# Twelve input projections moved from the joined attention-and-recurrence steps into a new stage with the memory's and samples' attentions

## The reference, cut to what matters

```python
SPLITS = (D_RNN, D_RNN, NSA_HEADS * NSA_HD, 3 * 2 * NSA_KV * NSA_HD, 3 * NSA_HEADS, MEM_HEADS * MEM_HD, N_BRANCH * D_MODEL)
def project(x, p):
    z = rmsnorm(x, p['norm_mix']) @ p['w_in']
    ...
    merge = jax.nn.sigmoid(mg.reshape(B, T, N_BRANCH, D_MODEL))
    return lru_x, lru_gate, q, cmp_kv, sel_kv, win_kv, nsa_gates, mem_q, merge
...
def prompt_layer(x, mem, table, p):
    lru_x, lru_gate, q, cmp_kv, sel_kv, win_kv, ngate, mq, merge = project(x, p)
    o_lru, conv_new, h_new = lru_branch(lru_x, lru_gate, ...)
    ...
    o_nsa = lax.map(block, jnp.arange(T // Q_BLOCK, dtype=jnp.int32))
    ...
    o_mem = mem_attend(mq, mkv)
    y = merge_ffn(x, o_lru, o_nsa, o_mem, merge, p)
```

## Time and profile before

| | us |
|---|---|
| median of 3 runs | 2673.55 (2670.8 to 2675.91) |
| the profiled execution | 2671.46 |
| its span | 2669.8 |
| joined steps (from 376.0) | to 1333.6 |
| last stage, to the tail's first matmul | 1333.6 to 1614.0 |
| tail | 1614.0 to the end |

### The profile page before, as it was taken

How to read it: one execution, slowest core, us unless ns; L and a number is a source line. 1 busy time by engine, 2 the same in 40 slices (tenths; PEclk the granted TensorE clock), 3 DMA queues, 4 the chain that set the end, 5 groups by cost and what they waited for, 6 DMA issues and landing times. The chain is left out here.

```text
span 2669.8 us, 37831 instructions
## 1 busy us (share of the span) xinstructions
PE 2416.7 (91%) x14415; PEld 2234.0 (84%) x14415; DVE 1072.0 (40%) x1945; ACT 724.7 (27%) x1319; POOL 655.0 (25%) x399
## 2 busy tenths in 40 slices
PE   7996877989989899899856587999999999999999
PEld 7995647789888788799733577999999999999999
DVE  5465014436255564655433003263333333333333
ACT  5222011242352544644332004232211111111111
POOL 2212001111111011010035001234444434433443
PEclk9997789999999899999678568999999999999999
DMA  5224424224233221110056626332111111111112
GB/s 178 88 80 168 125 72 147 67 67 128 64 97 88 74 63 52 60 49 28 6 125 181 160 65 246 104 119 91 61 48 47 40 47 47 47 39 47 47 47 79
DMA packets 136151, 226.26 MB, mean 85 GB/s; under 512 B 29418, under 2 KB 95098, under 8 KB 135420
## 3 DMA queue, kind: packets, MB, share of 16 engines
q1 hardware_dynamic: 122492, 194.57, 23.5%
q0 software_dynamic: 6560, 25.22, 3.2%
q10 hardware_dynamic: 6976, 4.79, 0.7%
HBM read 176.80 MB, written 55.08 MB: 87 GB/s over the span
## 5 line engine op out<-in xcount | busy, mean ns | idle before, releaser
L1101 PE MATMUL att_facc<-h_hi,att_w_hi 128*128 128x344 f32 x960 | 337.7, 352 | 57.8 <-DVE att_zf L1281 44.5
L2153 PE MATMUL tl_acc<-tl_x_hi,tl_w_hi 128*128 128x344 f32 x1632 | 348.0, 322 | 21.1 <-DVE tl_x_lo L2216 14.0
L2153 PE MATMUL tl_acc<-tl_x_lo,tl_w_hi 128*128 128x344 f32 x1632 | 347.2, 321 | 0.0
L2153 PE MATMUL tl_acc<-tl_x_hi,tl_w_lo 128*128 128x344 f32 x1632 | 345.4, 320 | 0.0
L1101 PE MATMUL att_facc<-h_lo,att_w_hi 128*128 128x344 f32 x960 | 314.5, 328 | 0.0
L1101 PE MATMUL att_facc<-h_hi,att_w_lo 128*128 128x344 f32 x960 | 314.2, 327 | 0.0
L2153 PEld LDWEIGHTS tl_acc<-tl_x_hi,tl_w_hi 128*128 128x128 f32 x1632 | 275.2, 189 | 22.5 <-issue 15.9
L2153 PEld LDWEIGHTS tl_acc<-tl_x_lo,tl_w_hi 128*128 128x128 f32 x1632 | 277.0, 189 | 0.0
L2153 PEld LDWEIGHTS tl_acc<-tl_x_hi,tl_w_lo 128*128 128x128 f32 x1632 | 272.6, 188 | 0.0
L2118 POOL TENSOR_TENSOR tl_w_lo<-tl_raw,tl_w_hi 128x1024 fp32r<-128x1024 f32 x64 | 153.9, 2404 | 425.1 <-ACT tl_w_hi L2059 425.1
L1101 PEld LDWEIGHTS att_facc<-h_hi,att_w_hi 128*128 128x128 f32 x960 | 187.7, 196 | 72.4 <-DVE att_zf L1281 42.2
(11 more groups left out here) (355 smaller groups left out, 4031.5 us busy)
## 6 DMA issues: line engine op xcount, KB each, us to landing
tl_raw<-in_w_ff SPq DMA_DIRECT2D x66, 512.0 KB, 3.6
z<-att_zf SPq DMA_DIRECT2D x120, 172.0 KB, 3.7
att_raw<-in_w_in SPq DMA_DIRECT2D x40, 512.0 KB, 4.3
tl_tmp<-z SPq DMA_DIRECT2D x24, 516.0 KB, 4.4
tl_raw<-in_w_up SPq DMA_DIRECT2D x16, 512.0 KB, 4.0
fr_raw<-in_w_in SPq DMA_DIRECT2D x14, 512.0 KB, 4.8
zn<-fr_x SPq DMA_DIRECT2D x10, 516.0 KB, 2.9
fr_x<-in_xT SPq DMA_DIRECT2D x8, 644.0 KB, 10.3
```

Source lines behind the costliest of these rows:

```text
L1101: mm = pe.matmul(facc[:, 0:CW], w[:, u % 2, k, :], h[:, k, c * CW:(c + 1) * CW], start=(x == 0), stop=(x == 23))
L2153: mm = pe.matmul(a[:, c, 0:CW], wt[:, s, k, :], x[:, x0, c * CW:(c + 1) * CW], start=first and n == 0, stop=last and n == 2)
```

## The change

- Of the 40 filler units 12 (`FILL`, 144 ticks) leave the joined steps; there 28 units (336 ticks) stay, dealt out as (3, 2) in turn in the first three query tiles and (2, 1, 1, 1) afterwards, done by about step 178. The weights of the first two of the 12 are loaded and split in the joined steps.
- Within a joined step TensorE now does values and transposes (and turns) ahead of the filler ticks; ScalarE does `copies` ahead of `probs`; VectorE does accumulate, maxima and coefficient ahead of the evictions.
- The 24 output copies move into the joined steps: GpSimd issues one in each of the steps 24 to 47.
- The last stage becomes one function, `memory_and_samples`, whose matmuls carry the 12 units as fillers: 4 ticks at its beginning, 2 in each of the 32 memory steps, 3 with the scores of each of the 8 sequences, 2 at the selection, 1 with each of 8 memory scores, 2 at the transposes, 3 with the values of each sequence, 2 with the memory values of each. They have the one PSUM bank 7 (`facc`). The memory attention's loop is written out.
- In this stage SyncE alone loads all pages, window keys and values, and memory keys and values of the samples, through a ring of ten slots in a fixed order (`ITEMS`); an item waits until its slot's former item has been read. SyncE has the constants too. ScalarE issues the later query tiles' loads and the stores of `o_mem`; GpSimd loads, splits and stores the fillers.

```diff
+FILL = 12
...
-    UNITS += list(range(U_MG, NU_IN))
-    NU = len(UNITS)
+    NU = len(UNITS) + NU_IN - FILL - U_MG
+    UNITS += list(range(U_MG, NU_IN - FILL + 2))
+    raw, w_hi, w_lo, zf = fill
     PRE = 24
-    TICKS = ((4,),) * 3 + ((2, 2, 2, 1, 1) * 4 + (2,) * 4,) * (QT - 3)
+    TICKS = ((3, 2),) * 3 + ((2, 1, 1, 1),) * (QT - 3)
...
+                if 0 <= J - COPY < len(copies):
+                    dst, src, slow = copies[J - COPY]
+                    pool.dma_start(dst, src, allow_slow_non_contiguous=slow).then_inc(c_out, 16)
...
-                for tick in ticks[J]:
-                    filler(tick)
                 if J >= 1:
                     values(J - 1)
                 transposes(J)
...
                     turn(J // NJ - 1, 1)
+                for tick in ticks[J]:
+                    filler(tick)
...
-                    if J + 1 < NST:
-                        probs(J + 1)
                     copies(J)
...
+                    if J + 1 < NST:
+                        probs(J + 1)
...
+                if 2 <= J < NST + 2:
+                    accumulate(J - 2)
+                if J < NST:
+                    maxima(J)
+                if 1 <= J <= NST:
+                    coefficient(J - 1)
                 for g in range(3 * NU):
                     if chunk_at[g] + 1 == J and J:
                         evict(g)
-                if J < NST:
-                    maxima(J)
-                if 2 <= J < NST + 2:
-                    accumulate(J - 2)
-                if 1 <= J <= NST:
-                    coefficient(J - 1)
...
+def memory_and_samples(nc, d, per, h_hi, h_lo, fill):
...
+    NR, NJ = 10, MH * QT
...
+    DEAL = {"begin": 4, "mat": 2, "ks": 3, "grp": 2, "km": 1, "turn": 2, "vs": 3, "vm": 2}
...
+    for b in range(0, NS, 2):
+        ITEMS += [("ks", b), ("ks", b + 1), ("kw", b)]
+    ITEMS += [("km", b) for b in range(NS)]
+    for b in range(0, NS, 2):
+        ITEMS += [("vs", b), ("vs", b + 1), ("vw", b)]
+    ITEMS += [("vm", b) for b in range(NS)]
...
+            def ring_load(i):
+                kind, b = ITEMS[i]
+                slot, landed = ring[:, i % NR], r_in[i % NR]
+                if i >= NR:
+                    was, of = ITEMS[i - NR]
+                    read = {"k": mk_mm if was == "km" else k_mm, "v": mo_mm if was == "vm" else o_mm}[was[0]]
+                    sp.wait_ge(read, of + (2 if was[1] == "w" else 1))
+                if kind in ("ks", "vs"):
...
+                    with sp.Fori(0, PAGES) as x:
+                        page = sp.value_load(pt[0:1, bass.ds(x + b * PAGES, 1)], min_val=0, max_val=src.shape[0] - 1)
...
+            for m in range(QT):
+                constants(m)
+                for i in range(loaded, min(NR, loaded + 2)):
+                    ring_load(i)
+                    loaded += 1
+            for i in range(loaded, len(ITEMS)):
+                ring_load(i)
...
             for j in range(NJ):
                 if j + 1 < NJ:
...
                     values(j - 1)
                 turn(j)
+                filler(("mat", j))
             values(NJ - 1)
...
+            for b in range(NS):
+                sample_scores(b)
+                filler(("ks", b))
...
+            for b in range(NS):
+                memory_scores(b)
+                filler(("km", b))
...
+            for b in range(NS):
+                sample_values(b)
+                filler(("vs", b))
...
+            for b in range(NS):
+                memory_values(b)
+                filler(("vm", b))
```

More of the change, by code:

```diff
@@ L1007, in _ @@
             q_low(0, 0)
-            for u in range(2, NU):
+            for u in range(2, NU + 2):
                 if unit_at[u - 2] == -1:
@@ L1405, in _ @@
                     evict(g)
-def memory_attention(nc, d, per, ctx, block, bank, between):
+def memory_and_samples(nc, d, per, h_hi, h_lo, fill):
+    raw, w_hi, w_lo, zf = fill
+    UNITS = list(range(NU_IN - FILL, NU_IN))
     SC = P ** -0.5
[L1414 to L1438, removed]
@@ new lines, in _, with filler @@
+        @block.tensor
+        def _(pe):
+            def filler(p):
+                for tick in ticks[p]:
+                    u, c, g, x0 = tick // 12, tick // 4 % 3, tick // 4, 6 * (tick % 4)
+                    if tick % 12 == 0 and u >= 2:
+                        pe.wait_ge(f_lo, u - 1)
+                    if x0 == 0 and g:
+                        pe.wait_ge(f_ev, g)
+                    for x in range(x0, x0 + 6):
+                        k = x // 3
+                        w, h = ((w_hi, h_hi), (w_hi, h_lo), (w_lo, h_hi))[x % 3]
+                        mm = pe.matmul(facc[:, 0:CW], w[:, u % 2, k, :], h[:, k, c * CW:(c + 1) * CW],
+                                       start=(x == 0), stop=(x == 23))
+                    if x0 == 18:
+                        mm.then_inc(f_mm, 1)
@@ new lines, in _, with chain, evict @@
+        @block.vector
+        def _(dve):
+            n = [0]
+            def chain(ins):
+                n[0] += 1
+                ins.then_inc(ch, 1)
+                dve.wait_ge(ch, n[0])
+            def evict(p):
+                for g in chunks[p]:
+                    if g >= 4:
+                        dve.wait_ge(f_out[g % 4], 16 * (g // 4))
+                    c = g % 3
+                    dve.wait_ge(f_mm, g + 1)
+                    dve.tensor_tensor(zf[:, g % 4], facc[:, 0:CW], per["rstd"][:, c * CW:(c + 1) * CW], ALU.mult).then_inc(f_ev, 1)
@@ new lines, in memory_queries @@
+            def memory_queries(part):
+                if part == 0:
+                    chain(dve.memset(mqb[:], 0.0))
+                    dve.wait_ge(mc_in, 16)
+                q0 = mqb[:].rearrange("p n c -> p (n c)")
+                for x in range(8 * part, 8 * part + 8):
+                    ins = dve.tensor_copy(q0[:, x * (RP + 1):x * (RP + 1) + 1], mqs[:, x % MH, x // MH:x // MH + 1])
+                if part == 3:
+                    ins.then_inc(mqb_done, 1)
+            evict(("begin", 0))
@@ new lines, in _ @@
+                if j:
+                    evict(("mat", j - 1))
+                if j == 16:
+                    sample_queries()
+                if j in (18, 20, 22, 24):
+                    memory_queries((j - 18) // 2)
+            evict(("mat", NJ - 1))
+            for b in range(NS - 1):
+                evict(("ks", b))
+            dve.wait_ge(k_mm, NS)
+            dve.wait_ge(b_in, 16 * 2 * NS)
+            chain(dve.tensor_copy(lc[:, 0:40], S3[0:RW, 2:42]))
+            chain(dve.tensor_tensor(lc[:, 40:NCMP], S3[0:RW, 42:2 + NCMP], b_cmp[:], ALU.add))
```

765 lines of the change are left out of this document (393 added, 372 removed).

## The result

The changed kernel takes 2701.75 us, the median of 19 runs, against 2673.03 for the kernel before on the same chips: ratio 1.0083, 95% interval 1.0059 to 1.0107. It is slower, outside the range of the prediction and on the other side. Its 19 times lie in two groups: 7 from 2678 to 2686 us, at a mean granted clock of 0.933 to 0.937, and 12 from 2695 to 2710, at 0.924 to 0.930. The kernel before has one group, 2667 to 2681. The profile of after is of the lower group (2678.02 us, span 2676.1); a second profile, of the upper group, is the first experiment.

The account below looks back on a forecast made before the run. TensorE was taken to bound the joined steps and the tail, with waits and a slow clock in the stage between. Joined steps -84 and last stage with gap +57 gave -27 from 2671.5: 2645 us, range 2600 to 2690.

Parts of the forecast that it names:

- Fillers taken out: Joined steps: 12 units, 144 ticks, leave; 136 us of PE work, thirds change by -102, -38 and +4 us.
- (a): Joined steps: 34 filler chunks ending inside a step's ticks lose 0.76 us each; 26 us, of which +20 taken.
- (b): Joined steps: scores-to-transposes chain of 3.2 us exceeds PE's 2.2 us cover in some steps; +20 us, bounds 0 and 50.
- (c): Joined steps: fewer ticks around the recurrence's sigmoid, square root and gelu; +12 us, bounds 0 and 30.
- (d): Joined steps: 24 more output copies on GpSimd are hidden; 0, at worst 10 us of late weights.
- (e): Last third of the joined steps: four more ticks cost PE 4 us but give a busier clock; 0 net.
- steps 1 to 3: Last stage: loads 13 us, memory attention until 128 us after the stage's start, last sample scores done at 174 us.
- E: Start of the last stage, at the end of the joined steps; times in that stage are counted from it.
- Step 5: Last stage: SyncE alone issues every page, 12.0 us an item; last window values land 276 us after the stage's start.
- Step 6: Last stage after the last page load: remaining values, transposes and memory values end 322 us after its start, +55 us.
- The gap: Between the last stage and the tail's first matmul: 14.0 us stays, +2 for the last filler's store.
- R2: Joined steps: chain over VectorE and ScalarE, not PE, becomes the bound; -50 there, +67 in last stage: 2688, chance 0.22.

Follow-up runs that it names:

- the first experiment: The changed kernel unaltered, run again for a second profile: 2704.23 us over four runs, the profile at 2706.29.
- the aligned ticks: Changed kernel with joined-step ticks (2, 2, 4) in the first three query tiles and (2, 1, 1) after, chunks ending with a step's last tick: 2705.7 us.

## Why the prediction was wrong

- **Fillers taken out (-136).** Right as work; TensorE's busy time fell by 117 only. The step that failed is the assumption behind it, that what remains runs at the old clock. No term of the sum stood for a lower clock in the first three tiles (0.98 to 0.92). It is 17 to 19 us, all that the steps gave back less than forecast (66 for 84).
- **(a) Evictions (+20).** Right. The places were as counted (27 and 6, for 27 and 7). The page's 44.5 and 52.5 hold waits for the recurrence too; without those over 1.5 us, the waits behind evictions in the steps went from 7.8 us to 27.1, by 19. Not all of it could be won back, as the aligned ticks showed.
- **(b) The chain (+20).** Right: 1.12 us in the wait shown, at 34 steps, 37.1 us in all, less the 14.3 that the values no longer wait for copies: +23.
- **(c) The recurrence (+12).** Waits of fillers or values over 1.5 us behind VectorE, which itself had stood behind the recurrence: nine places before and after, 28.7 and 33.8 us: +5. Idle time in all grew by 51 us, for 52 predicted. That the sum agrees so closely is in part luck, as (b) and (c) miss in opposite directions.
- **(d) Copies (0).** Right.
- **(e) The last tile (0 net).** 102.0 us in after against 96.3: four more ticks, with the new order, raised the clock from 0.77 to 0.79 only. The thought that ticks give the clock back was right, but not with four more: it came with 24 in the tile (90.3 us at 1.00), and spreading them was the largest gain of any single edit here.
- **Last stage, steps 1 to 3.** Right: memory scores at E + 13.1, sample scores at E + 127, the last scores done at E + 175 (128 and 174 predicted).
- **Step 5, pages.** Right within 6 us: last window at 1549.37, E + 282 (276 predicted). Splitting the pages between two issuing engines took 13.6 us off. By the Trainium skill, "DMA: Bandwidth & Descriptors", section "Issuing engines are not separate DMA queues", it would have saved the sequencer's time alone, which it calls usually small; here that time was the bound, and the row decided rightly.
- **Step 6.** Wrong: 46 us predicted behind the last page, 52 in the lower group (1549.37 to 1601.86), 77 in the upper. I had put 2.5 us for the slow clock "behind the waits"; in the upper group the clock stays low in the memory values without any wait. That is 24 us in 12 of 19 runs.
- **The gap.** 18.0 us instead of the 16.
- **The sum.** Joined steps -66 instead of -84, last stage and gap +72 instead of +57: +6 for the lower group; with 24 more for the upper one +30, near the median's +29. R2 had the sign, but not the mechanism: its mark, transposes waiting in nearly every step, was met at 34 of 192, and fillers taken out still gave back time. Its price, 2688, lay below the median, since it had no clock either, and the +67 in it for the last stage came from no step. The range ended at R2. The hard end of the joined steps, -50, was added up wrongly: with (a) at 20 and (b) to (d) at their hard bounds it is -136 + 20 + 50 + 30 + 10 = -26, and R2 would have stood at 2712, above the median.

What stays open: how the idle time and the lower clock share the loss in the first three tiles; no run held one while it changed the other. Why the memory values take the higher clock in some runs and the lower in others is open: the trace shows when the clock turns, not why.

## What to carry to other kernels

Before wide matmuls are moved out of a stage, read the granted clock of every stretch that has few of them, and price what remains at that clock; here a tile with 24 ticks was faster than with none. In this kernel filler paid most where the kernel's own matmuls are narrow, spread evenly. A sum of engine work bounds the gain only until the chain of one step is reached: leaving most of the filler out took 245 us of matmuls away and brought 65.

## What the runs showed of the hardware

TensorE's clock can stay low without any idle time that the profile shows. In the kernel before, the memory values, 128 matmuls of one column each, take 25.85 us, all of it busy, at 0.53:

```profile
1574.21:1600.06 25.85, 25.85 (x128) 25.77 (x128) 0.00 (x0) 0.00 (x0) 2.87 (x4) 0.53 0.28 82
```

In the changed kernel, with twelve wide matmuls behind every sixteen of them, the engine is busy 54.27 of 54.27 us at 0.51, after a stretch at 0.65, or 31.21 of 31.21 at 0.95, after one at 0.66; with 24 wide ones it was 0.96 in the profile, and no run of ten lies in the upper group. The Trainium skill, "TensorE: Matmul & The Clock Gate", section "HAM oscillation — how this bites in real kernels", names idle gaps of the engine as what throws the clock back; by that alone a stretch without idle time would be at 2.4 GHz but for its beginning. In the upper group it was at 1.2 GHz nearly throughout (0.51), so here the measurement decides: with more wide matmuls among the narrow ones the stretch kept the higher clock, with the engine busy all the time in both.
